# Routing weights of the expert rows: one-hot products on TensorE in place of a scatter and a reload

## The chip, the cores and the metric

The kernel runs on one NeuronCore of a Trainium2 chip. The metric is the device time of one execution in microseconds (us). Each core has five engines with a queue of their own: TensorE (PE in the profile; PEld is its weight load), VectorE (DVE), ScalarE (ACT), GpSimd (POOL) and SyncE (SP), which here only starts transfers. Engines wait for each other through semaphores; each works through its queue in order.

## The reference, cut to what matters

One encoder layer on 544 tokens (512 of one request, 32 of another): a mixer, then a mixture of experts on the normalised rows. The change touches only the second part.

```python
gl = t @ w_group + b_group                      # 4 groups
gp = softmax(gl); g_idx = top_k(gl, 1)
p_g = gp[g_idx]
el_sel = (t @ w_erouter[g_idx] + b_erouter)     # 4 experts of the group
top_v, top_i = top_k(el_sel, 2)
w2 = softmax(top_v) * p_g                       # two weights per token
expert_id = g_idx * 4 + top_i
combine = sum(one_hot(expert_id, 16) * w2[..., None])
for e in range(16):
    hid = silu(t @ w_gate[e]) * (t @ w_up[e])
    out = out + combine[:, e:e + 1] * (hid @ w_down[e])
```

Every token has two experts and two weights, `w1` and `w2` in the kernel. All is float32.

## The kernel before, in words

**Tiles.** The rows of one expert are gathered into a tile of 128 rows; an expert with more rows than that gets extra tiles. There are 16 tiles, one per expert, and up to 8 extra; `last`, read at run time, is the index of the last tile. Tile `i` has for each of its rows (a *slot*) a token and a routing weight. Tokens of slots are in `ids`, weights in `slot_w`, both with slots on the 128 partitions and tiles in the columns. The token of a slot is found by TensorE: VectorE makes a one-hot row of the token's rank within its tile (`at_rank`) and a one-hot of the tile times the token's number (`at_tile`, `at_extra`, all bf16), and the product of both over the tokens gives the numbers. The slot's weight goes another way: VectorE works out the address `w_at` = rank x 32 + tile (`weight_places`), POOL scatters the weights one element at a time to `w_dram` (the loop at L785 to L789, ten transfers: five token tiles times two choices), and after all have landed reloads the table into `slot_w` (L792). `w_dram` was zeroed early by a transfer of SP (L531).

**Work on a tile.** Weights of an expert come as six chunks of 1 MB (0, 1 gate; 2, 3 up; 4, 5 down). float32 products are made of three passes over rounded high and low parts (`three_passes`, L463), so for each chunk ACT makes the high part (`high_chunk`, L1089), VectorE the low part (`low_chunk`, L1988, 128x2048 elements), and when VectorE is done with a chunk SP loads the next tile's into the same place. For tile `i`:

- POOL: `gather(i)` fetches the tile's 128 rows (L767 copies the index, L762 sends the indirect transfer), once TensorE has transposed the tile before.
- TensorE: `turn_rows` transposes the gathered rows (L1509), `gate_up` makes gate and up products (48 matmuls), `turn_hidden` transposes the hidden rows (L1542), `down` makes the output rows (24 matmuls). `turn_rows(n)` and `turn_hidden` names count from tile 0, `turn_rows(1)` being tile 0's; `down(i)` is the down product of tile i - 1 and runs behind `gate_up(i)`.
- ACT: sigmoid of the gate (`gate`, L1112), high parts of transposed rows (L1098) and hidden rows (L1116), and `result(i)`: the output rows of tile i - 1 times `slot_w` (L1105), then a transfer of them to memory (L1108).
- VectorE: gate (L2114), `hidden` (L2119), low parts of rows (`rest_of_rows`, L2109) and of hidden rows (`rest_of_hidden`, L2123).

**What sets the order.** It is written out by hand for each engine. Tiles 0 and 1 are written out (`stage(0)`, `stage(1)`), tiles from 2 on run in a loop over `stage(i)`. Routing is finished while tiles 0 and 1 are under way: in VectorE's list `choice_weights` (the weights w1, w2), `extra_places`, `weight_places` and `extra_rows` stand between the chunks of tiles 0 and 1. In `stage(1)` ACT leaves `result(1)` out; it comes behind the stage, after a wait for the reload:

```python
            stage(1)
            act.wait_ge(w_moved, 16 * (2 * J + 1))
            result(1)
```

In the loop, `down(i)` on TensorE waits for `y_ready`, that is for ACT to have read the output rows of the tile before. At the end (L2194) VectorE waits for the reload once more, and POOL gathers every token's two rows and adds them to the residual (L806).

## Time and profile before

| | |
|---|---|
| median of 3 runs | 1048.53 us (1047.71 to 1052.13) |
| the profiled execution, its own time | 1052.81 us |
| its span, first to last instruction | 1050.7 us |
| mean granted clock of TensorE in it | 0.969 of full speed |
| busy: PE, DVE, ACT, POOL | 972.4, 674.0, 547.8, 288.1 us |
| chain that ended last, by engine | PE 43%, POOL 4%, DVE 3%, DMA 3% |
| of it, L788 (the scatter) and its reload | 2%, 1% |

A profile is one execution. Busy time says how long an engine worked, not whether anything waited for it. The idle time of an engine is put down to what ended it. The chain is followed back from the last instruction to what released each step. `PJ<-MEM_R 128*128 128x512` reads: written to PJ from MEM_R, 128 by 128 weights, 128 partitions by 512 elements.

### The profile page before, as it was taken

Reading aid. Unit: us, or ns where it says so; the run is one execution under the profiler, and the core shown is the slowest. Engines: PE = TensorE matmul, PEld = TensorE weight load, DVE = VectorE, ACT = ScalarE, POOL = GpSimd, SP = SyncE. Lnnn points to the kernel's source line nnn. Section 1 sums busy time; section 2 is a strip of 40 time slices with the busy share of each in tenths; the row PEclk is TensorE's granted clock in tenths of the full one; section 3 lists DMA queues with packets and bytes.
Section 4 is the critical chain, followed back from the end, with each engine's and each line's share of the span. In section 5 each row is a group of like instructions: output and inputs, shape, how many; then the busy total and the mean of one; then the engine's idle time right before and its main releaser. Section 6 shows DMA issues by size and latency. Waiting matters only on the chain.

```text
span 1050.7 us, 16726 instructions
## 1 busy us (share of the span) xinstructions
PE 972.4 (93%) x5963; PEld 856.7 (82%) x5963; DVE 674.0 (64%) x865; ACT 547.8 (52%) x610; POOL 288.1 (27%) x189
## 2 busy tenths in 40 slices
PE   5999899999999998899999999949779999999984
PEld 3999789889978986799999987737668888888873
DVE  5495659767865974622111114389598989898975
ACT  5645525825542572323333323457388787878752
POOL 1013214312421441533443443005400101011161
PEclk9999999999999999899999999969989999999998
DMA  9552222303222220233233269139899999999986
GB/s 294 172 169 70 53 57 60 105 20 91 79 59 58 58 76 4 61 86 95 80 85 94 80 206 310 61 135 315 330 356 396 413 413 414 412 412 413 384 205 171
DMA packets 146951, 193.20 MB, mean 184 GB/s; under 512 B 14936, under 2 KB 92158, under 8 KB 146788
## 3 DMA queue, kind: packets, MB, share of 16 engines
q1 hardware_dynamic: 139434, 166.34, 46.0%
q0 software_dynamic: 5008, 16.23, 5.2%
q10 hardware_dynamic: 2474, 10.18, 2.5%
q8 instruction: 21, 0.34, 0.1%
q14 instruction: 14, 0.11, 0.0%
HBM read 172.93 MB, written 19.79 MB: 183 GB/s over the span
## 4 chain that ended last, share of the span: by engine, by line
PE 43%; POOL 4%; DVE 3%; DMA 3%; issue 3%; SPq 2%; ACT 1%; ACTq 0%; DVEq 0%; POOLq 0%
PE PJ L463 40%; POOL slot_weights L788 2%; POOL MEM L806 2%; PE MS L1509 1%; SPq L609 1%; DMA MEM<-expert_rows,MEM 1%; PE NM L1457 1%; DMA MEM<-slot_weights 1%; PE NM L1542 1%; DMA RAW<-in_w_out_dram 0%; DMA MEM<-t_rows,MEM 0%; DVE MEM L2215 0%; POOL MEM_R L684 0%; DVE MEM_R L1988 0%; PE MS L1448 0%
## 5 line engine op out<-in xcount | busy, mean ns | idle before, releaser
L463 PE MATMUL PJ<-MEM_R 128*128 128x272 f32 (+2 forms) x5016 | 807.1, 322 | 11.6 <-DVE MEM_R L2109 3.4
L463 PEld LDWEIGHTS PJ<-MEM_R 128*128 128x128 f32 x5016 | 726.0, 192 | 75.7 <-issue 10.0
L684 POOL TENSOR_TENSOR MEM_R<-RAW,MEM_R 128x1024 fp32r<-128x1024 f32 x72 | 178.8, 2492 | 319.6 <-ACT MEM_R L831 319.6
L1988 DVE TENSOR_TENSOR MEM_R<-CHUNK,MEM_R 128x2048 fp32r<-128x2048 f32 x100 | 224.5, 2285 | 26.2 <-ACT MEM_R L1089 26.0
L1089 ACT CAST MEM_R<-CHUNK 128x2048 fp32r<-128x2048 f32 x100 | 189.3, 1912 | 12.5 <-PE PJ L463 8.0
L831 ACT CAST MEM_R<-RAW 128x1024 fp32r<-128x1024 f32 x81 | 84.3, 1048 | 130.4 <-DMA RAW<-in_w_pb_dram 42.9
L1901 DVE TENSOR_TENSOR MERGED<-PJ,MEM 128x544 f32<-128x544 f32 x16 | 11.6, 725 | 143.4 <-PE PJ L463 132.3
L767 POOL COPY MEM<-MEM 128x1 uint32 (+1 forms) x16 | 19.6, 1222 | 223.2 <-PE MS L1509 223.2
L1731 DVE SCALAR_TENSOR_TENSOR MEM<-MEM 128x548 f32<-128x548 f32 x72 | 58.9, 818 | 8.5 <-DVE MEM L1729 0.9
L1098 ACT CAST MEM_R<-MS 128x1024 fp32r<-128x1024 f32 x17 | 17.3, 1018 | 33.2 <-PE MS L1509 33.2
L888 ACT COPY MEM<-PJ 128x272 f32<-128x272 f32 x24 | 9.0, 376 | 45.8 <-PE PJ L463 45.8
L1105 ACT ACTIVATE MEM<-PJ,MEM 128x1024 f32<-128x1024 f32 x15 | 16.8, 1119 | 26.5 <-PE PJ L463 13.3
L895 ACT ACTIVATE MEM<-MEM 128x548 f32<-128x548 f32 x16 | 10.6, 664 | 38.1 <-DVE MEM L1731 38.0
L762 POOL DMA_INDIRECT MEM<-t_rows,MEM x18 | 19.3, 1075 | 26.4 <-POOL MEM L767 12.6
L1299 PE MATMUL MS<-MEM 128*128 128x512 f32 (+4 forms) x80 | 22.1, 420 | 4.5 <-DVE MEM L1771 4.4
L908 ACT ACTIVATE MEM<-NM 128x1024 f32<-128x1024 f32 x4 | 4.1, 1025 | 41.9 <-DVE M_Y L1805 41.9
L1745 DVE TENSOR_TENSOR MEM<-MEM 128x548 f32<-128x548 f32 x8 | 5.8, 730 | 30.4 <-ACT MEM L952 30.4
L1509 PE MATMUL MS<-MEM 128*128 128x128 f32 x136 | 18.5, 281 | 7.0 <-DMA MEM<-t_rows,MEM 7.0
L1509 PEld LDWEIGHTS MS<-MEM 128*128 128x128 f32 x136 | 16.5, 146 | 9.3 <-issue 7.4
L1299 PEld LDWEIGHTS MS<-MEM 128*128 128x128 f32 (+1 forms) x80 | 12.5, 189 | 14.0 <-DVE MEM L1771 7.7
L806 POOL DMA_INDIRECT MEM<-expert_rows,MEM x10 | 20.0, 1998 | 10.3 <-DMA expert_rows<-MEM 7.5
L1800 DVE SCALAR_TENSOR_TENSOR MEM<-MS,MEM 128x512 f32<-128x512 f32 x4 | 2.8, 692 | 30.4 <-PE MS L1327 30.4
(324 smaller groups left out, 947.2 us busy)
## 6 DMA issues: line engine op xcount, KB each, us to landing
CHUNK<-in_w_gate_dram SPq DMA_DIRECT2D x34, 1024.0 KB, 7.1
CHUNK<-in_w_up_dram SPq DMA_DIRECT2D x34, 1024.0 KB, 8.8
CHUNK<-in_w_down_dram SPq DMA_DIRECT2D x34, 1024.0 KB, 8.0
RAW<-in_w_in_dram SPq DMA_DIRECT2D x56, 512.0 KB, 3.7
expert_rows<-MEM ACTq DMA_DIRECT2D x15, 512.0 KB, 6.0
expert_rows<-MEM SPq DMA_DIRECT2D x10, 512.0 KB
RAW<-in_w_pa_dram SPq DMA_DIRECT2D x8, 512.0 KB, 3.6
RAW<-in_w_pb_dram SPq DMA_DIRECT2D x8, 512.0 KB, 3.6
```

The costliest lines, as they stand in the source:

```text
L463: ins = pe.matmul(out, w(a), x(b), start=first and n == 0, stop=last and n == 2)
L684: tt(lo, raw[slot], hi.bitcast(F32), ALU.subtract).then_inc(lo_done, 1)
L762: pool.indirect_dma_start(out=xg, out_offset=None, in_=t_dram, in_offset=bass.IndirectOffsetOnAxis(ap=index, axis=0)).then_inc(xg_in, 16)
L767: pool.tensor_copy(idcur[:, 0:1], ids[:, ds(col, 1)]).then_inc(steps_p, 1)
L788: pool.indirect_dma_start(out=w_dram, out_offset=bass.IndirectOffsetOnAxis(ap=w_at[0:n, m, j:j + 1], axis=0), in_=w[0:n, j:j + 1], in_offs ...
L806: pool.indirect_dma_start(out=x2[0:n, j, :], out_offset=None, in_=y_dram, in_offset=bass.IndirectOffsetOnAxis(ap=slot_i[0:n, m, j:j + 1], ...
L831: act.copy(hl[slot][0], raw[slot]).then_inc(hi_done, 1)
L1089: act.copy(moe_hl[c][0], moe_raw[c]).then_inc(chunk_hi[c], 1)
L1299: last = pe.matmul(b[0:rows_of[j], 0:n], k[:, ct, keys_of(j)], q[:, ct, quer], start=ct == 0, stop=ct == CT - 1)
L1509: last = pe.transpose(MS[:, half, P * m:P * m + P], xg[:, (4 * half + m) * P:(4 * half + m + 1) * P], ident)
L1731: ins = stt(dst, buf[:, tap:tap + LN_], cw[tap], dst, ALU.mult, ALU.add)
L1988: tt(moe_hl[c][1], moe_raw[c], moe_hl[c][0].bitcast(F32), ALU.subtract).then_inc(chunk_lo[c], 1)
```

## The change

The weights' table is made the way of the tokens' numbers. A weight is cut into three bf16 parts (its rounding, the rounding of what is left, and again), the one-hot of the tile is multiplied by each of the parts (`at_weight`, 3 x 26 columns for each token tile and choice), and ten bf16 matmuls with the one-hot of the rank (`at_place`) sum them over the tokens. VectorE adds the three parts up from PSUM into `slot_w`. The scatter, the reload, the table in memory, its zeroing and the addresses are gone.

- POOL makes the parts (five instructions of 10 elements, each waiting for the one before) and the three products, behind `stage(0)` and ahead of `stage(1)`.
- TensorE: `slot_weights`, behind `gate_up(1)`, ahead of `turn_rows(3)` and `down(1)`.
- VectorE: `is_tile` has 26 columns a token and choice instead of 10; `weight_places` goes; `place_weights` comes behind `low_chunk(5, 0)`.
- ACT: `result(1)` moves into `stage(1)`, ahead of `turned_hidden(1)`.
- TensorE's `down` no longer waits for `y_ready`: it waits for `hidT_ready`, which ACT and VectorE give only after `result`.
- `at_place` and `at_weight` lie where the output rows `yt` lie later.

```diff
+        w12 = small(2, J)
+        w1, w2 = w12[:, 0], w12[:, 1]
...
-        slot_w = small(WT)
+        slot_w = small(TAB)
...
-            sp.dma_start(w_dram.rearrange("(p t) a -> p (t a)", p=P), zeros[:, 0:WT]).then_inc(rows_zeroed, 16)
...
             stage(0)
-            pool.wait_ge(rows_zeroed, 16 * (EXTRA + 4))
+            pool.wait_ge(weights_ready, 1)
+            pool.tensor_copy(w_third[:, 0], w12).then_inc(w_split, 1)
+            pool.wait_ge(w_split, 1)
+            tt(w_left, w12, w_third[:, 0], ALU.subtract).then_inc(w_split, 1)
+            pool.wait_ge(w_split, 2)
+            pool.tensor_copy(w_third[:, 1], w_left).then_inc(w_split, 1)
+            pool.wait_ge(w_split, 3)
+            tt(w_left, w_left, w_third[:, 1], ALU.subtract).then_inc(w_split, 1)
+            pool.wait_ge(w_split, 4)
+            pool.tensor_copy(w_third[:, 2], w_left).then_inc(w_split, 1)
+            pool.wait_ge(w_split, 5)
             pool.wait_ge(weights_ready, 2)
-            for j in ORDER:
-                n = rows_of[j]
-                for m, w in enumerate((w1, w2)):
-                    pool.indirect_dma_start(out=w_dram, out_offset=bass.IndirectOffsetOnAxis(ap=w_at[0:n, m, j:j + 1], axis=0),
-                                            in_=w[0:n, j:j + 1], in_offset=None).then_inc(w_moved, 16)
+            for k in range(3):
+                tt(at_weight[:, :, :, k, :], is_tile, w_third[:, k].unsqueeze(3).to_broadcast([P, 2, J, TAB]), ALU.mult).then_inc(w_split, 1)
             stage(1)
-            pool.wait_ge(w_moved, 16 * 2 * J)
-            pool.dma_start(slot_w, w_dram.rearrange("(p t) a -> p (t a)", p=P)).then_inc(w_moved, 16)
...
-                if not isinstance(i, int):
-                    result(i)
+                if isinstance(i, int):
+                    act.wait_ge(weights_ready, 3)
+                result(i)
                 turned_hidden(i)
                 high_chunk(5, i)
 
             stage(1)
-            act.wait_ge(w_moved, 16 * (2 * J + 1))
-            result(1)
...
+            def slot_weights():
+                pe.wait_ge(w_split, 8)
+                for m in range(2):
+                    for j in range(J):
+                        n = rows_of[j]
+                        last = pe.matmul(NM[:, 1, 0:3 * TAB], at_place[0:n, m, j, :], at_weight[0:n, m, j].rearrange("p k t -> p (k t)"),
                                          start=m + j == 0, stop=m == 1 and j == J - 1)
                 last.then_inc(slots_done, 1)
...
-                if not isinstance(i, int):
-                    await_step(pe, y_ready, i)
                 pe.wait_ge(hidT_ready, i)
...
             gate_up(1)
+            slot_weights()
             turn_rows(3)
...
-                L(tt(is_extra, iox, spread2(t12, NX), ALU.is_equal))
+                L(tt(is_tile, iox, spread2(t12, TAB), ALU.is_equal))
+                dve.sem_inc(weights_ready, 1)
...
-            def weight_places():
-                L(stt(x12, r12, float(WT), t12, ALU.mult, ALU.add))
-                dve.tensor_copy(w_at, x12).then_inc(weights_ready, 1)
...
+            def place_weights():
+                dve.wait_ge(slots_done, 3)
+                dve.tensor_reduce(slot_w, NM[:, 1, 0:3 * TAB].rearrange("p (k t) -> p t k", k=3), AX.X, ALU.add).then_inc(weights_ready, 1)
...
-            weight_places()
             low_chunk(1, 1)
...
             low_chunk(5, 0)
+            place_weights()
...
-            dve.wait_ge(w_moved, 16 * (2 * J + 1))
```

What stands on three engines, with the lines of the respective kernel (a line of the kernel before moves down by 6 to 18 in the changed one). POOL's queue before, from the gather of `stage(0)` on:

```order
L767 COPY MEM<-MEM 128x1 [waits xT_full]
L762 DMA MEM<-t_rows,MEM 128x1024 [waits steps_p]
L788 DMA slot_weights<-MEM 4096x1 [waits weights_ready,rows_zeroed]
L788 DMA slot_weights<-MEM 4096x1 x9
L792 DMA MEM<-slot_weights 128x32 [waits w_moved]
```

Between the last two stand the copy and the gather of `stage(1)`, in rows like the first two. The same place in the changed kernel (W is `w_third`, SB is `at_weight`):

```order
L768 DMA MEM<-t_rows,MEM 128x1024 [waits steps_p]
L790 CAST W_66<-MEM 128x10 [waits weights_ready]
L792 TENSOR_TENSOR MEM<-MEM,W_66 128x10 [waits w_split]
L794 CAST W_66<-MEM 128x10 [waits w_split]
L796 TENSOR_TENSOR MEM<-MEM,W_66 128x10 [waits w_split]
L798 CAST W_66<-MEM 128x10 [waits w_split]
L802 TENSOR_TENSOR SB<-MEM,W_66 128x10x26 [waits weights_ready,w_split]
L802 TENSOR_TENSOR SB<-MEM,W_66 128x10x26 x2
L773 COPY MEM<-MEM 128x1 [waits xT_full]
```

Ten transfers and a reload have become eight instructions that read and write SBUF; the gather of `stage(1)` stands behind them as it stood behind the scatter. VectorE in the changed kernel, from `rest_of_rows(2)` to `hidden(1)` (L2005 is `low_chunk`, L2107 the new reduction):

```order
L2127 TENSOR_TENSOR MEM_R<-MS,MEM_R 128x1024 [waits xT_hi]
L2005 TENSOR_TENSOR MEM_R<-CHUNK_60,MEM_R 128x2048 [waits chunk_hi1]
L2005 TENSOR_TENSOR MEM_R<-CHUNK_61,MEM_R 128x2048 [waits chunk_hi2]
L2111 COPY MEM<-PJ 128x10 [waits slots_done]
L2112 TENSOR_TENSOR MEM<-PJ,MEM 128x10 [waits steps_v]
L2005 TENSOR_TENSOR MEM_R<-CHUNK_62,MEM_R 128x2048 [waits steps_v,chunk_hi3]
L2141 TENSOR_TENSOR MEM_R<-NM,MEM_R 128x512 [waits hT_hi]
L2005 TENSOR_TENSOR MEM_R<-CHUNK_63,MEM_R 128x2048 [waits chunk_hi4]
L2005 TENSOR_TENSOR MEM_R<-CHUNK_64,MEM_R 128x2048 [waits chunk_hi5]
L2107 TENSOR_REDUCE MEM<-NM 128x26 [waits slots_done]
L2005 TENSOR_TENSOR MEM_R<-CHUNK_59,MEM_R 128x2048 [waits chunk_hi0]
```

Before, two 10-element instructions stood ahead of the first L2005 row (then L1988), and the reduction was not there: now all of VectorE's work for tile 2 stands behind a wait for TensorE. ACT at the end of `stage(1)` in the changed kernel (L1116 is the output rows' scaling, L1127 `turned_hidden`, L1100 `high_chunk`):

```order
L1100 CAST MEM_R<-CHUNK_63 128x2048 [waits chunk_used4,chunk_in4]
L1116 ACTIVATE MEM<-PJ,MEM 128x1024 [waits y_out,weights_ready,chunk_used5]
L1119 DMA expert_rows<-MEM 128x1024 [waits y_ready]
L1127 CAST MEM_R<-NM 128x512 [waits hT_full]
L1100 CAST MEM_R<-CHUNK_64 128x2048 [waits chunk_used5,chunk_in5]
```

Before, the scaling and its transfer stood behind the last of these rows and waited for `w_moved`.

## Rows read from the trace of the kernel before

**Rows 1.** The head of the page.

```profile
span 1050.7 us, 16726 instructions
```

**Rows 2.** The chain that ended last, 748 to 799 us: start, us, what.

```profile
748.32 6.96 DMA MEM<-slot_weights
...
755.42 1.12 ACT MEM L1105
...
781.41 0.87 PE MS L1509 x8
782.28 5.58 PE PJ L463 x24
787.86 0.44 PE NM L1542 x4
788.29 10.91 PE PJ L463 x48
```

**Rows 3.** The waits of ACT from 690 us: total, times, longest (us).

```profile
ACT MEM L1105 <- DMA MEM<-slot_weights: 13.2, 1, 13.2
```

**Rows 4.** The timeline, TensorE: start, us, line, shapes, [idle before, releaser].

```profile
718.96 11.18 PE L463 MATMUL PJ<-MEM_R 128*128 128x512 f32 x48 [0.25 <-DVE MEM_R L2109]
...
739.16 0.66 PE L1542 MATMUL NM<-MEM 128*128 128x128 f32 x4 [2.58 <-DVE MEM L2119]
...
740.60 12.76 PE L463 MATMUL PJ<-MEM_R 128*128 128x512 f32 x48 [0.78 <-DVE MEM_R L2109]
...
755.26 1.06 PE L1509 MATMUL MS<-MEM 128*128 128x128 f32 x8 [1.90 <-DMA MEM<-t_rows,MEM]
...
756.83 5.83 PE L463 MATMUL PJ<-MEM_R 128*128 128x512 f32 x24 [0.51 <-ACT MEM L1105]
...
767.96 1.12 PE L1542 MATMUL NM<-MEM 128*128 128x128 f32 x4 [5.30 <-DVE MEM L2119]
```

**Rows 5.** Stretches: busy of PE, PEld, DVE, ACT, POOL, then clock, DMA share, GB/s.

```profile
740.60:753.40 12.80, 12.76 (x48) 10.07 (x48) 7.77 (x9) 1.64 (x1) 7.20 (x5) 0.87 1.04 405
753.40:756.80 3.40, 1.06 (x8) 0.86 (x9) 0.00 (x0) 1.11 (x1) 0.18 (x1) 1.00 0.36 143
756.80:762.70 5.90, 5.83 (x24) 4.44 (x24) 2.69 (x2) 4.63 (x4) 0.99 (x1) 1.00 0.54 178
762.70:769.00 6.30, 1.04 (x4) 0.72 (x4) 6.30 (x6) 6.30 (x5) 0.00 (x0) 0.66 0.82 275
...
781.50:800.00 18.50, 18.50 (x93) 15.45 (x91) 16.65 (x11) 14.28 (x10) 1.92 (x2) 1.00 1.04 406
```

**Rows 6.** The timeline, VectorE and POOL.

```profile
719.10 4.49 DVE L1988 TENSOR_TENSOR MEM_R<-CHUNK,MEM_R 128x2048 fp32r<-128x2048 f32 x2
...
722.46 1.87 POOL L788 DMA_INDIRECT slot_weights<-MEM  x1 [0.30 <-issue]
...
726.82 6.69 DVE L1988 TENSOR_TENSOR MEM_R<-CHUNK,MEM_R 128x2048 fp32r<-128x2048 f32 x3
...
727.47 2.48 POOL L788 DMA_INDIRECT slot_weights<-MEM  x1 [0.30 <-issue]
...
745.50 2.81 POOL L762 DMA_INDIRECT MEM<-t_rows,MEM  x1 [0.82 <-POOL MEM L767]
```

**Rows 7.** Single lines (ns min/median/max), then two matmul groups (us, mean ns).

```profile
L684 POOL TENSOR_TENSOR MEM_R<-RAW,MEM_R x72: 2345/2396/4055, 75.2 to 644.5; 128x1024 fp32r<-128x1024 f32 x72
L1731 DVE SCALAR_TENSOR_TENSOR MEM<-MEM x72: 787/790/2816, 53.6 to 370.5; 128x548 f32<-128x548 f32 x72
L767 POOL COPY MEM<-MEM x16: 181/1405/1407, 716.8 to 996.2; 128x1 uint32 x14, 128x1 uint32<-128x1 uint32 x2
L2070 DVE TENSOR_TENSOR MEM<-MEM x1: 253/253/253, 714.0 to 714.0; 128x100 f32<-128x100 f32 x1
...
L1501 PE MATMUL PJ<-AT 128*128 128x20 bf16 (+1 forms) x10 | 0.7, 174 | 0.0
L1484 PE MATMUL NM<-AT 128*128 128x80 bf16 (+4 forms) x5 | 0.5, 228 | 0.0
```

More of the change, by code:

```diff
@@ L82, in hawk_mlstm_hmoe_kernel @@
     TAB = TILES + 2
-    WT = 32
     EPS = 1e-6
@@ L121, in hawk_mlstm_hmoe_kernel @@
         y_dram = dram("expert_rows", [TILES * P + 1, D], F32)
-        w_dram = dram("slot_weights", [P * WT, 1], F32)
         rows_dram = dram("gate_rows", [2 * H * N + H * LS], F32)
@@ L303, in hawk_mlstm_hmoe_kernel @@
         lg, chosen = small(J, NR), small(J, NG, EG)
-        gmax, gidx, pg, w1, w2, dv = (small(J) for _ in range(6))
+        gmax, gidx, pg, dv = (small(J) for _ in range(4))
+        w12 = small(2, J)
+        w1, w2 = w12[:, 0], w12[:, 1]
         v12, i12, e12, r12, x12, q12, t12, a12 = (small(2, J) for _ in range(8))
@@ L328, in hawk_mlstm_hmoe_kernel @@
         assert bf0 + (J + 1) * NE <= 2 * 2 * N and NX <= NE
-        is_extra = late(J * D, 2, J, NX)
         slot_i = small(2, J).bitcast(U32)
@@ L332, in hawk_mlstm_hmoe_kernel @@
         last_i = small(1).bitcast(I32)
-        w_at = small(2, J).bitcast(U32)
-        slot_w = small(WT)
+        slot_w = small(TAB)
         sel_id = small(2)
+        is_tile = small(2, J, TAB)
+        w_left = small(2, J)
+        small(-o[0] % 8)
+        w_third = nc.alloc_sbuf_tensor_at("W3", [P, 6 * J], BF16, offset=base + 4 * (cuts["xh"] + o[0])).rearrange("p (k m j) -> p k m j", k=3, m=2)
+        small(3 * J)
+        s_words = nc.alloc_sbuf_tensor_at("SB", [P, 4 * N], BF16, offset=base + 4 * cuts["sig"])
+        at_place = s_words[:, 0:2 * J * P].rearrange("p (m j n) -> p m j n", m=2, j=J)
+        at_weight = s_words[:, 2 * J * P:2 * J * (P + 3 * TAB)].rearrange("p (m j k t) -> p m j k t", m=2, j=J, k=3)
+        assert 2 * J * (P + 3 * TAB) <= 4 * N
         ids = small(TAB).bitcast(U32)
@@ L797, in _ @@
                     stage(i)
-            pool.wait_ge(weights_ready, 3)
+            pool.wait_ge(weights_ready, 4)
             await_step(pool, y_out, last * 16)
@@ L1011, in _ @@
                 sigmoid_qk(hd, 3)
-                act.wait_ge(rows_zeroed, 16 * (EXTRA + 4))
+                act.wait_ge(rows_zeroed, 16 * (EXTRA + 3))
                 second_part(hd, (5,))
@@ L1106, in result @@
                                scale=slot_w[:, ds(i - 1, 1)]).then_inc(y_ready, 1)
-                act.wait_ge(y_ready, i + 1)
+                act.wait_ge(y_ready, i)
                 act.dma_start(y_dram[ds(i * P - P, P), :], yt).then_inc(y_out, 16)
@@ L1119, in _ @@
             act.sem_inc(y_out, 16)
-            act.sem_inc(y_ready, 1)
             turned_rows(1)
@@ L1500, in extra_slots @@
                         n = rows_of[j]
-                        last = pe.matmul(PJ[:, 2, 0:2 * NX], at_rank[m][0:n, j, :], at_extra[0:n, m, j, :],
+                        last = pe.matmul(PJ[:, 2, 0:2 * NX], at_place[0:n, m, j, :], at_extra[0:n, m, j, :],
+                                         start=m + j == 0, stop=m == 1 and j == J - 1)
+                last.then_inc(slots_done, 1)
+            def slot_weights():
[4 more added lines that the diff above has]
+                        last = pe.matmul(NM[:, 1, 0:3 * TAB], at_place[0:n, m, j, :], at_weight[0:n, m, j].rearrange("p k t -> p (k t)"),
                                          start=m + j == 0, stop=m == 1 and j == J - 1)
```

8 lines of the change are left out of this document (4 added, 4 removed).

## The prediction

> **What bounds the kernel now.** I read the page's head first, then the waits, then the chain that ended last, and last the timeline around the chain's odd stretch. The profiled execution took 1052.81 us, its span is 1050.7 [rows 1], so 2.1 us lie around the span; it is 4.3 above the median of the runs, 1048.53. A gain in the span is taken off the median as it stands.
>
> From tile 3 on TensorE does nothing but expert tiles, with no wait between them: gate_up 10.91, turn_rows 0.87, down 5.58, turn_hidden 0.44, together 17.80 us a tile [rows 2]. That part runs at TensorE's own pace and the change does not touch it. The odd stretch is ahead of it. ACT sits idle for 13.2 us until the routing weights have come back from memory [rows 3], and the reload alone is 6.96 us of the chain [rows 2]. ACT is in order, so all casts of the next tile stand behind that wait, VectorE's differences behind the casts, and hidden(2) behind those.
>
> What counts is what TensorE loses [rows 4]: 1.90 us before turn_rows(4), whose gather POOL issued late because it was still sending the scatter; about 0.5 before down(2); 5.30 before turn_hidden(2), which waits for hidden(2) on VectorE. After that the granted clock shows 0.66 for 762.7 to 769.0 [rows 5], that is a stretch at 1.2 instead of 2.4 GHz, and TensorE is through gate_up(3) only at 781.41 [rows 2]. An earlier stall, 2.58 and 0.78 us around turn_hidden(1), is caused by VectorE's backlog, not by the weights; behind it gate_up(2) takes 12.76 us [rows 4] where later ones take 10.91, at a mean clock of 0.87 [rows 5].
>
> **What is taken away.** Ten scatters and one reload leave POOL's queue, one zero fill leaves SP's, and with them ACT's 13.2 us. If nothing else moved, gate_up(2) would start at 740.60 as now, and TensorE would run through without waiting: 740.60 + 12.76 + 0.87 + 5.58 + 0.44 + 10.91 = 771.16 in place of 781.41, a gain of 10.2 us. I checked the cover: VectorE is through low_chunk(5, 1) at 747.4 and base_places at 748.6; three L1988 of 2.24 [rows 6] and two 512-column instructions of 0.7 put hidden(2) at 756.7, 16.1 us after gate_up(2) starts, and down(2) ends after 19.2. The zero fill was long finished and nothing waits for it by name: nothing. TensorE's wait for y_ready in down: its order is kept by hidT_ready, it stood idle for ACT once, 0.5 us, which is in the sum.
>
> **What is added, and where it stands.** POOL now splits w12 into three bf16 parts in five chained instructions of 10 elements, then makes three products of 260 elements. TensorE's ten matmuls (slot_weights) wait for the last product and stand ahead of turn_rows(3) and down(1). VectorE's place_weights waits for those matmuls and stands ahead of low_chunk(0, 2), so all of VectorE's work for tile 2 is behind it. Thus if POOL is late, both engines stop.
>
> Is POOL late? Row by row the scatters show when POOL gets at SBUF while VectorE runs L1988 (two inputs in SBUF). L1988 in a run of two from 719.10 ends at 723.59; the scatter begun at 722.46 ends at 724.33, 0.74 later. In the run of three from 726.82 a border lies near 729.06; the scatter begun at 727.47 ends at 729.95, 0.89 behind it [rows 6]. Seven of the other eight follow the same pattern; one, at 739.66, meets no L1988 and takes 0.97 in all. So a POOL instruction waits for the L1988 that is running and gets in at the border. The reverse is in the trace too: L1731 takes 790 ns but up to 2816, L684 on POOL 2396 but up to 4055 [rows 7]. By the Trainium skill, SBUF — State Buffer, section "SBUF: two separate sides", VectorE and GpSimd have one SBUF port pair in common, held as a lock for a whole instruction, the loser being blocked; by that rule the gain is cut, without it the 10.2 above would stand. The trace agrees, with the borders just given.
>
> The walk, in times of the trace before: POOL's gather(2) is issued by 718.7, then the chain starts. VectorE starts low_chunk(1, 1) about 718.9 (before at 719.10, since weight_places' two small instructions went) and runs five L1988 up to about 731.1, with short gaps for extra_rows and rest_of_hidden(0). Each of the five small POOL instructions is 0.18 us free and up to 1.41 when held [rows 7]. It gets in at a border (721.2, 723.4, 726.1, 728.9) or in one of the gaps, and either way the fifth is done by 728.9 to 729.1. A product: L684 is 2.34 ns an element, so 260 elements are 0.61 us; with the 0.18 of a tiny copy as its fixed part, 0.79 [rows 7]. Either the first product gets in at 728.9 and holds low_chunk(5, 0) back by 0.79, and the other two follow it, or all three start at 731.1; both end at 733.5. TensorE's ten matmuls of 78 columns lie between 174 ns each (20 columns) and 228 (80 columns, at the low clock) [rows 7]; issued back to back they overlap, and I take 0.8 for all: 734.3. VectorE's reduction of 78 elements is like the 0.25 of L2070 [rows 7]; done at 734.6 with its semaphore. low_chunk(0, 2) then starts near 734.7 instead of 731.3: **3.4 us late**. is_tile grows from 100 to 260 elements, some 0.15 us by the one nanosecond an element of VectorE, beside ACT's turned_rows(2), for which VectorE waits anyway: nothing.
>
> Who pays these 3.4 us: hidden(1), so turn_hidden(1) at 742.6 in place of 739.16, and gate_up(2) at 744.0 in place of 740.60. TensorE itself is ready earlier: 734.3 + 0.9 + 5.8 = 741.0 (gate_up(1) ends at 730.1 as before, 718.96 + 11.18 [rows 4]). ACT's result(1) now stands ahead of turned_hidden(1); it needs the end of down(1), 741.0, takes 1.12 [rows 2] and a DMA issue, and is done at 742.6, before turned_hidden(1) can start: hidden. POOL's gather(3) was issued from 745.50 on [rows 6] and its rows were used at 755.26 [rows 4], 9.8 later; now its copy can go at 735.3 and the gather some 2.2 later, so the rows are there by 747.3, and turn_rows(4) needs them at 756.8: hidden, the 1.90 us are gone.
>
> **Sum.** 10.2 - 3.4 = 6.8 us: gate_up(3) ends near 774.6. 1048.53 - 6.8 = **1041.7 us** (the profiled execution's own time: 1046.0, its span 1043.9). About 0.5%, 5.2 us, is what a measurement of this kernel tells from no change. Bounds: were POOL never held, 10.2, and 12.1 if the shorter stall before gate_up(2) also leaves the clock up (12.76 becomes 10.91). Downward: a product could take up to L684's full 2.4 us, if operands with repeated elements are slow; three add 4.8, which leaves 2.0. The new idle of TensorE, 730.1 to 733.5, may bring a low stretch of its own: 1.85 us by gate_up(2)'s excess, of which 1.6 is covered, since down(1) ends 1.6 ahead of hidden(1).
>
> **Rivals.**
> - *POOL is in time* (it finishes before 730, say because small instructions slip into gaps two at a time). Then gain 10.2 to 12.1: 1036.4 to 1038.3. For: the gap before low_chunk(3, 1) and the one at rest_of_hidden(0). Against: five chained plus three, and five L1988 in the way. Chance 0.17.
> - *The loads bound it.* In 740.6 to 753.4 the DMA share is 1.04 at 405 GB/s, as in 781.5 to 800 (1.04, 406). If loads set the pace, only idle DMA time can be won back: 0.64 x 3.4 + 0.46 x 5.9 + 0.18 x 6.3 = 6.0 us [rows 5], less the 3.4 by which VectorE frees buffers later: 2.6, so 1045.9. Against: TensorE waits for no load from 781 on, and its pieces add up to the period. Chance 0.10.
> - *The chain on POOL is longer than priced* (slow products). Gain 2.0 to 5, around 1045. Chance 0.13.
> - *Slower: the clock.* The new stall puts TensorE at 1.2 GHz and it stays there through down(1) and gate_up(2). down(1) ends near 746.8, gate_up(2) starts at 747.7 and takes 21.8 us (2 x 10.91): 769.5 against 756.8, 12.7 lost against 6.8 won, 1054.4. It decides if the low stretch outlasts down(1) by more than half of gate_up(2). Against: in gate_up(2) of before the mean is 0.87, so the low part is about a quarter of it [rows 5]. Chance 0.05.
> - *Forecast* as summed: 0.55.
>
> **How the numbers follow.** Faster by over 0.5% (below 1043.3): all of the first rival, 0.17, most of the forecast, 0.47 of 0.55, a little of the loads and the long chain, 0.06: 0.70. Within 0.5%: the rest of these, 0.25. Slower: 0.05. The range takes in the rivals but the last and the far ends: 1037.0 to 1046.0.
>
> **What would show it.** Right: no slot_weights DMA; ACT's 13.2 us wait gone; POOL's small instructions ending at the borders of VectorE's L1988, the last product near 733 to 734 when the start of gate_up(1) is laid on 718.96; TensorE idle 3 to 4 us before the 78-column matmuls; VectorE idle before its reduction; turn_hidden(2) with no wait. Wrong: the products done before gate_up(1) ends (gain of 10), products of over 1 us each free of VectorE (gain below 5), or a granted clock of 0.50 through all of gate_up(2).

## The result and the profile after

| | before | changed |
|---|---|---|
| median | 1048.53 us (1045.78 to 1052.45, 7 runs) | 1039.01 us (1036.23 to 1043.74, 7 runs) |
| the profiled execution | 1052.81 us | 1038.45 us |

The ratio is 0.9906, 95% interval 0.988 to 0.9932: 9.5 us between the medians, 7 to 12.6 by the interval. The forecast was 6.8 us and 1041.7, just outside that interval. The sign held, and so did the account of what is taken away; the size was short by a third, because the account of the cost failed. The head of the changed kernel's page:

```profile
span 1036.5 us, 16724 instructions
```

The spans differ by 14.2 us, more than the medians do. 3.8 of it lie ahead of gate_up(1), which started at 718.96 and now starts at 715.13. In the profiles of this study that start lies anywhere from 712.2 to 719.9, in kernels that differ little up to there, so I count from the start of gate_up(1) in each profile. TensorE's timeline of the changed kernel (start, us, line, shapes, idle time before it; L1519 is `slot_weights`, L1527 `turn_rows`, L1558 `turn_hidden`, L470 the products of `gate_up`, x48, and `down`, x24):

```profile
715.13 12.81 PE L470 MATMUL PJ<-MEM_R 128*128 128x512 f32 x48
727.78 0.84 PE L1519 MATMUL NM<-SB 128*128 128x78 bf16 x10
...
736.76 0.66 PE L1558 MATMUL NM<-MEM 128*128 128x128 f32 x4 [1.53 <-DVE MEM L2137]
738.20 11.16 PE L470 MATMUL PJ<-MEM_R 128*128 128x512 f32 x48 [0.78 <-DVE MEM_R L2127]
749.20 1.04 PE L1527 MATMUL MS<-MEM 128*128 128x128 f32 x8
749.99 5.83 PE L470 MATMUL PJ<-MEM_R 128*128 128x512 f32 x24
755.65 0.60 PE L1558 MATMUL NM<-MEM 128*128 128x128 f32 x4
756.17 11.19 PE L470 MATMUL PJ<-MEM_R 128*128 128x512 f32 x48
767.20 1.03 PE L1527 MATMUL MS<-MEM 128*128 128x128 f32 x8
```

Beside [rows 4]: the 1.90 us before turn_rows(4) and the 5.30 before turn_hidden(2) are gone (749.20 and 755.65 have no idle time), the 2.58 before turn_hidden(1) has become 1.53. gate_up(3) ends, and the transposes behind it start, 52.07 us after the start of gate_up(1); before it was 62.29. These are **10.2 us**, and from there to the end both profiles take the same (269.45 before, 269.30 now). So the whole gain lies in these two tiles, as forecast. It is a net figure, of one execution on each side: the one of before took 4.3 us more than its median.

ACT's waits from 686 us on:

```profile
ACT MEM L1116 <- PE PJ L470: 14.9, 15, 1.0
ACT MEM_R L1100 <- DMA CHUNK<-in_w_up_dram: 9.6, 14, 1.1
```

The 13.2 us of [rows 3] are gone. What is new is the second row: chunk loads now land 10 to 11.6 us after their issue in the median where it was 7 to 9, and ACT waits for one a tile, up to 1.1 us. Two tiles of the chain that ended last show that none of it reaches TensorE, whose 0.87, 5.58, 0.44 and 10.91 are those of [rows 2]:

```profile
802.98 0.87 PE MS L1527 x8
803.85 5.58 PE PJ L470 x24
809.43 0.44 PE NM L1558 x4
809.87 10.91 PE PJ L470 x48
```

Now the two queues on which the forecast's 3.4 us rested. POOL, from gather(2) to gather(3):

```profile
713.97 0.96 POOL L768 DMA_INDIRECT MEM<-t_rows,MEM  x1 [0.79 <-POOL MEM L773]
714.93 0.21 POOL L790 CAST W<-MEM 128x10 bf16<-128x10 f32 x1
715.22 2.14 POOL L792 TENSOR_TENSOR MEM<-MEM,W 128x10 f32<-128x10 f32 x1
717.43 2.13 POOL L794 CAST W<-MEM 128x10 bf16<-128x10 f32 x1
719.64 0.20 POOL L796 TENSOR_TENSOR MEM<-MEM,W 128x10 f32<-128x10 f32 x1
719.90 0.19 POOL L798 CAST W<-MEM 128x10 bf16<-128x10 f32 x1
720.18 5.76 POOL L802 TENSOR_TENSOR SB<-MEM,W 128x260 bf16<-128x260 f32 x3
...
731.94 2.83 POOL L768 DMA_INDIRECT MEM<-t_rows,MEM  x1 [0.79 <-POOL MEM L773]
```

and VectorE in the same time:

```profile
714.99 4.51 DVE L2005 TENSOR_TENSOR MEM_R<-CHUNK,MEM_R 128x2048 fp32r<-128x2048 f32 x2
719.43 0.15 DVE L2111 COPY MEM<-PJ 128x10 f32<-128x10 f32 x1
...
719.94 2.30 DVE L2005 TENSOR_TENSOR MEM_R<-CHUNK,MEM_R 128x2048 fp32r<-128x2048 f32 x1 [0.15 <-DVE MEM L2112]
722.16 0.68 DVE L2141 TENSOR_TENSOR MEM_R<-NM,MEM_R 128x512 fp32r<-128x512 f32 x1
722.76 5.32 DVE L2005 TENSOR_TENSOR MEM_R<-CHUNK,MEM_R 128x2048 fp32r<-128x2048 f32 x2
728.67 0.24 DVE L2107 TENSOR_REDUCE MEM<-NM 128x26 f32<-128x78 f32 x1 [0.58 <-PE NM L1519]
728.82 2.28 DVE L2005 TENSOR_TENSOR MEM_R<-CHUNK,MEM_R 128x2048 fp32r<-128x2048 f32 x1
```

L792 and L794 are held for 2.1 us each and end at the borders of the two L2005 from 714.99 (near 717.3 and 719.5), as forecast. But L790 got in before that pair began, and L796 and L798 both started in the half microsecond of L2111 and L2112, in which VectorE runs no instruction with two inputs in SBUF. The first product started 0.24 us too late for that gap:

```profile
720.18 2.55 POOL L802 TENSOR_TENSOR SB<-MEM,W 128x260 bf16<-128x260 f32 x1
```

It was held by the L2005 from 719.94. The second took 0.62 us beside L2141, which has an input in PSUM, and the third, 2.67 us, was held again. The three products end at 725.94, 10.8 us after gate_up(1) started; the forecast was 14.5. They hold VectorE's pair L2005 at 722.76 for 0.84 us in all (5.32 in place of 4.48). At 727.78 TensorE finds its operands waiting. VectorE idles 0.58 us for TensorE, not for POOL, and starts low_chunk(0, 2) 13.7 us after the start of gate_up(1), before 12.3: **1.4 us late, not 3.4**.

The clock: TensorE in slices of 1 us (length, busy, instructions, granted clock, DMA share, GB/s):

```profile
715.00:716.00 1.00, 1.00 (x7) 1.00 0.74 240
716.00:717.00 1.00, 1.00 (x4) 0.55 0.79 313
717.00:718.00 1.00, 1.00 (x4) 0.50 0.49 201
718.00:719.00 1.00, 1.00 (x4) 0.50 0.69 55
719.00:720.00 1.00, 1.00 (x5) 0.74 0.77 229
```

There is one stretch at 1.2 GHz, inside gate_up(1), which takes 12.81 us; gate_up(2) takes 11.16. Before it was the other way round, 11.18 and 12.76 [rows 4].

### The profile page after: what moved, and what is told of

It is laid out like the page before. It is cut to its first block, busy times and chain, and to the rows that moved or that the text cites. A ratio compares the mean times of both kernels' runs of the same rounds, so it can differ in the third digit from the quotient of the medians.

```text
span 1036.5 us, 16724 instructions
## 1 busy us (share of the span) xinstructions
PE 968.3 (93%) x5973; PEld 854.3 (82%) x5973; DVE 673.2 (65%) x864; ACT 548.6 (53%) x610; POOL 278.7 (27%) x186
## 4 chain that ended last, share of the span: by engine, by line
PE 72%; DVE 13%; issue 6%; ACT 4%; SPq 2%; DMA 2%; DVEq 1%; POOL 0%; ACTq 0%; POOLq 0%
PE PJ L470 60%; DVE MEM L1748 2%; PE NM L1326 2%; PE PJ L1275 2%; PE MS L1527 1%; DVE MEM L1849 1%; PE MS L1346 1%; PE MS L1308 1%; SPq L615 1%; DVE MEM_R L2005 1%; DMA MEM<-in_x_prompt_dram 1%; PE NM L1466 1%; PE NM L1558 1%; PE MS L1336 1%; DVE MEM_R L1658 1%
## 5 line engine op out<-in xcount | busy, mean ns | idle before, releaser
L470 PE MATMUL PJ<-MEM_R 128*128 128x272 f32 (+2 forms) x5016 | 804.4, 321 | 10.2 <-DVE MEM_R L2127 3.1
L470 PEld LDWEIGHTS PJ<-MEM_R 128*128 128x128 f32 x5016 | 723.8, 191 | 72.9 <-issue 9.0
L690 POOL TENSOR_TENSOR MEM_R<-RAW,MEM_R 128x1024 fp32r<-128x1024 f32 x72 | 176.2, 2455 | 318.9 <-ACT MEM_R L842 318.9
L2005 DVE TENSOR_TENSOR MEM_R<-CHUNK,MEM_R 128x2048 fp32r<-128x2048 f32 x100 | 225.4, 2293 | 15.6 <-ACT MEM_R L1100 14.3
L1100 ACT CAST MEM_R<-CHUNK 128x2048 fp32r<-128x2048 f32 x100 | 189.3, 1912 | 16.8 <-DMA CHUNK<-in_w_up_dram 9.6
L1918 DVE TENSOR_TENSOR MERGED<-PJ,MEM 128x544 f32<-128x544 f32 x16 | 11.6, 724 | 141.5 <-PE PJ L470 132.2
L773 POOL COPY MEM<-MEM 128x1 uint32 (+1 forms) x16 | 22.2, 1385 | 222.8 <-PE MS L1527 222.8
L768 POOL DMA_INDIRECT MEM<-t_rows,MEM x18 | 20.7, 1150 | 26.4 <-POOL MEM L773 12.6
L1116 ACT ACTIVATE MEM<-PJ,MEM 128x1024 f32<-128x1024 f32 x15 | 16.8, 1119 | 14.9 <-PE PJ L470 14.9
L1308 PEld LDWEIGHTS MS<-MEM 128*128 128x128 f32 (+1 forms) x80 | 12.3, 185 | 14.6 <-DVE MEM L1788 7.8
L1527 PE MATMUL MS<-MEM 128*128 128x128 f32 x136 | 18.6, 282 | 5.2 <-DMA MEM<-t_rows,MEM 5.2
L1527 PEld LDWEIGHTS MS<-MEM 128*128 128x128 f32 x136 | 16.5, 146 | 7.2 <-issue 5.3
## 6 DMA issues: line engine op xcount, KB each, us to landing
CHUNK<-in_w_up_dram SPq DMA_DIRECT2D x34, 1024.0 KB, 11.6
```

Of the source, the lines that this page charges most:

```text
L470: ins = pe.matmul(out, w(a), x(b), start=first and n == 0, stop=last and n == 2)
L690: tt(lo, raw[slot], hi.bitcast(F32), ALU.subtract).then_inc(lo_done, 1)
L768: pool.indirect_dma_start(out=xg, out_offset=None, in_=t_dram, in_offset=bass.IndirectOffsetOnAxis(ap=index, axis=0)).then_inc(xg_in, 16)
L773: pool.tensor_copy(idcur[:, 0:1], ids[:, ds(col, 1)]).then_inc(steps_p, 1)
L1100: act.copy(moe_hl[c][0], moe_raw[c]).then_inc(chunk_hi[c], 1)
L1308: last = pe.matmul(b[0:rows_of[j], 0:n], k[:, ct, keys_of(j)], q[:, ct, quer], start=ct == 0, stop=ct == CT - 1)
```

## The experiments

"Mark" is the time from the start of gate_up(1) to the transposes behind gate_up(3) in the run's profile; "turn" that to turn_hidden(1). The ratio is to the kernel before, run alongside; e1 and e5 do not compute the reference's output.

| run | median us | ratio to before, 95% interval | turn | mark |
|---|---|---|---|---|
| before | 1048.5 | | 20.20 | 62.29 |
| changed | 1039.0 | 0.9906 (0.988 to 0.9932) | 21.63 | 52.07 |
| changed, again | 1039.9 | 0.9907 (0.9882 to 0.9932) | 21.63 | 52.07 |
| e1 no wait on ACT | 1043.5 | 0.9934 (0.991 to 0.9957) | 20.20 | 56.64 |
| e2 result(1) behind stage(1) | 1039.1 | 0.9909 (0.9882 to 0.9936) | 20.96 | 54.08 |
| e3 chain ahead of stage(0) | 1041.8 | 0.9929 (0.9909 to 0.9949) | 21.47 | 53.31 |
| e4 products twice | 1042.2 | 0.9936 (0.9917 to 0.9955) | 23.90 | 54.33 |
| e5 half the scatters | 1039.0 | 0.9895 (0.9871 to 0.992) | 20.20 | 52.07 |
| e6 split on VectorE | 1041.9 | 0.9921 (0.9898 to 0.9944) | 22.14 | 54.78 |
| e7 slot_weights in the gap | 1039.9 | 0.991 (0.9882 to 0.9939) | 20.81 | 52.34 |
| e9 e7 and extra_slots earlier | 1040.5 | 0.9917 (0.9891 to 0.9944) | 20.82 | 52.33 |
| e10 e9 with filled gap | 1039.1 | 0.99 (0.9875 to 0.9926) | 21.42 | 51.40 |
| e11 scatter kept, wait moved | 1044.6 | 0.9962 (0.9944 to 0.998) | 20.21 | 54.47 |

The intervals are 4 to 6 us wide in all, so 1 us is told apart by the profiles alone, and each profile is one execution: that of e1 was the slowest of its seven (1049.42), that of e4 the fastest of its six (1039.32), that of e11 the second of twelve (1040.41). Theory A throughout: what was lost stood behind ACT's wait for the reload and behind POOL's queue of scatters; what is paid is the end of POOL's new chain, as far as it outlasts gate_up(1), and what VectorE does ahead of hidden(1).

### Where the loss was: e1, e5, e11

e1 keeps scatter and reload and takes ACT's wait away:

```diff
-                               scale=slot_w[:, ds(i - 1, 1)]).then_inc(y_ready, 1)
+                               scale=ones[:, ds(i - 1, 1)]).then_inc(y_ready, 1)
...
             stage(1)
-            act.wait_ge(w_moved, 16 * (2 * J + 1))
             result(1)
...
+            act.wait_ge(w_moved, 16 * (2 * J + 1))
             act.wait_ge(chunk_used[5], last)
```

> The kernel before, but output rows of all tiles save the last two are scaled by ones instead of the routing weights (so the output is not the reference's), and ACT waits for the reload only ahead of the last two tiles; the ten scatters and the reload stay on POOL. Theory A (the loss is ACT standing still for the reload, with all casts behind it): ACT's 13.2 us wait and TensorE's 5.3 us before turn_hidden(2) vanish, the 1.9 us before turn_rows(4) stay since POOL still sends its scatters first; gain over before 7 to 9 us, about 1040.5. Rival B (POOL's late gather or the scatters' traffic is the larger part): gain below 4 us, 1045 or more.

Measured: 0.9934, about 6.9 us, just below the 7 to 9 expected (4.5 to 9.5 by the interval); the mark is 5.65 us earlier than before, 4.6 later than in the changed kernel. TensorE's timeline of e1:

```profile
755.87 1.94 PE L1509 MATMUL MS<-MEM 128*128 128x128 f32 x8 [3.25 <-DMA MEM<-t_rows,MEM]
757.47 7.82 PE L463 MATMUL PJ<-MEM_R 128*128 128x512 f32 x24
```

The 5.3 us before turn_hidden(2) are gone. The wait for gather(3) is 3.25 us, longer than before's 1.90, because gate_up(2) was quicker here, and a low stretch of the clock follows it: 1.94 for transposes that take 1.03, 7.82 for a down that takes 5.83. So the late gather, which I priced at 1.90, costs 3.2 + 0.9 + 2.0 = 6.1 us here; less the 1.4 by which turn_hidden(1) is earlier than in the changed kernel, that is the difference of the marks. ACT's wait was the larger part of the loss, POOL's queue the rest. Rival B falls.

e5 leaves out the scatters of the second choice:

```diff
-                for m, w in enumerate((w1, w2)):
+                for m, w in ((0, w1),):
...
-            pool.wait_ge(w_moved, 16 * 2 * J)
+            pool.wait_ge(w_moved, 16 * J)
```

(and the two waits for the reload count J + 1 in place of 2 * J + 1).

> The kernel before, scattering only the weights of the first choice, so the rows of every second expert get weight zero (the output is not the reference's): five scatters instead of ten. Theory A (ACT and gather(3) wait for POOL's queue, about 2.3 us a scatter): POOL is free some 11.5 us earlier, gather(3) is in time, and the reload lands near the moment ACT is ready, so ACT's wait falls from 13.2 to about 2 us; most of the change's gain appears, 7 to 9 us, about 1041. Rival F (the loss sits in the reload's latency and the waits' order, not in the number of scatters): gain below 4 us.

Measured: 0.9895, 11 us (8.4 to 13.6 by the interval), more than the 7 to 9 expected. The mark, 52.07, is that of the changed kernel, but the equality is chance: turn_hidden(1) is 1.4 us earlier and gate_up(2) took 12.77 us in place of 11.16. ACT's waits, POOL's gather(3) and TensorE's timeline of e5:

```profile
ACT MEM L1105 <- DMA MEM<-slot_weights: 1.0, 1, 1.0
```

```profile
728.83 2.82 POOL L762 DMA_INDIRECT MEM<-t_rows,MEM  x1 [0.81 <-POOL MEM L767]
```

```profile
747.68 1.03 PE L1509 MATMUL MS<-MEM 128*128 128x128 f32 x8
748.47 5.83 PE L463 MATMUL PJ<-MEM_R 128*128 128x512 f32 x24
754.14 0.60 PE L1542 MATMUL NM<-MEM 128*128 128x128 f32 x4
```

No idle time before turn_rows(4) and turn_hidden(2). Nothing but five scatters has gone; scatter to memory, reload and the old order are all there. The method of the kernel before was not slow because it goes through memory. It was slow because ten scatters take 2.3 us each, held by L1988 as [rows 6] show, and gather(3) and the reload stand behind all ten: with five fewer, gather(3) is issued 15.4 us after the start of gate_up(1) (728.83 - 713.42) in place of 26.5, 11.1 us earlier, and of ACT's 13.2 us 1.0 is left. Rival F falls.

e11 keeps the scatter whole and moves ACT's wait into stage(2), behind the gate of tile 2 and three casts (the expectation says four):

```diff
+                if isinstance(i, int) and i == 2:
+                    act.wait_ge(w_moved, 16 * (2 * J + 1))
+                    result(1)
                 turned_rows(i + 2)
...
             stage(1)
-            act.wait_ge(w_moved, 16 * (2 * J + 1))
-            result(1)
+            stage(2)
...
-            with act.Fori(2, TILES) as i:
+            with act.Fori(3, TILES) as i:
```

> The kernel before with its scatter and reload, only that ACT's wait for the reload and result(1) stand in stage(2), behind four casts and the gate of tile 2 instead of ahead of them. Theory A (the loss is the work queued behind ACT's wait, and POOL's late gather beside it): TensorE's 5.3 us before turn_hidden(2) vanish, the 1.9 to 3.3 us before turn_rows(4) stay; gain over before 5 to 8 us, about 1043, near e1. Rival K (the weights must be there, wherever the wait stands): down(2) waits for result(1) as long as ACT did, gain below 3 us.

Measured: 0.9962, a gain of 4.0 us (2.1 to 5.9 by the interval) where 5 to 8 were expected, a miss; the profile's mark is 7.8 us earlier than before. TensorE's timeline of e11:

```profile
748.68 1.07 PE L1511 MATMUL MS<-MEM 128*128 128x128 f32 x8 [1.29 <-DMA MEM<-t_rows,MEM]
750.44 5.82 PE L463 MATMUL PJ<-MEM_R 128*128 128x512 f32 x24 [0.69 <-ACT MEM L1105]
756.10 0.60 PE L1544 MATMUL NM<-MEM 128*128 128x128 f32 x4
```

As expected the 5.30 is gone. 1.29 and 0.69 are left; 1.9 to 3.3 were expected before turn_rows(4), and the 0.69 before down(2) not at all. ACT still waits 2.4 us for the reload, and the later place has a price of its own: result(2) waits 3.6 us until result(1) has been sent from the same buffer, which held no matmul in this execution. The profile and the medians disagree by 3.8 us, for which I have no row: the profiled execution is one of the two quickest, and the others may hold longer waits. That the place of the wait matters is shown; how much of the gain a mere reordering brings is open between 2 and 8 us. Rival K, a gain below 3 us, is not excluded by the runs; its mechanism, down(2) waiting as long as ACT did, is not what the profile shows.

### What is paid: e4, e2, e6, e3

e4 makes the three products a second time, into the same place, and TensorE waits for the second set:

```diff
-            for k in range(3):
+            for n, k in enumerate((0, 1, 2) * 2):
+                if n == 3:
+                    pool.wait_ge(w_split, 8)
                 tt(at_weight[:, :, :, k, :], is_tile, w_third[:, k].unsqueeze(3).to_broadcast([P, 2, J, TAB]), ALU.mult).then_inc(w_split, 1)
...
-                pe.wait_ge(w_split, 8)
+                pe.wait_ge(w_split, 11)
```

> The changed kernel with the three products made twice, the second set behind the first and TensorE waiting for it. Theory A (the end of POOL's chain is the price: both TensorE and VectorE wait for it): the chain ends near 15 us after the start of gate_up(1) instead of 10.8, VectorE starts low_chunk(0, 2) 2 to 2.5 us later, TensorE idles before the 78-column matmuls; 2 to 4 us slower than the changed kernel, about 1041.5. Rival E (hidden anyway, the stall before turn_hidden(1) swallows it): within 0.5 us of it.

Measured: 0.9936, 3.1 us slower than the changed kernel by the ratios. TensorE's timeline of e4:

```profile
726.88 1.12 PE L1521 MATMUL NM<-SB 128*128 128x78 bf16 x10 [3.46 <-POOL SB L804]
727.93 1.97 PE L1529 MATMUL MS<-MEM 128*128 128x128 f32 x8
729.55 6.21 PE L470 MATMUL PJ<-MEM_R 128*128 128x512 f32 x24
736.14 0.66 PE L1560 MATMUL NM<-MEM 128*128 128x128 f32 x4 [0.37 <-DVE MEM L2139]
```

This is the case that the prediction described: the chain ends 14.6 us after the start of gate_up(1), TensorE idles 3.46 us for POOL, turn_hidden(1) is 2.3 us later than in the changed kernel, and the mark too. So what the prediction put behind the end of the chain is right for a chain of that length; in the changed kernel the chain was shorter. Rival E falls. The idle spell also brings a low stretch, but it lies in the ten matmuls, the transposes (1.97) and the start of down(1) (6.21), where the wait before turn_hidden(1) covers it, as the prediction had it.

e2 undoes the other part of the change: result(1) behind stage(1), and down's wait for y_ready (with the counts of y_ready that go with it).

```diff
-                if isinstance(i, int):
-                    act.wait_ge(weights_ready, 3)
-                result(i)
+                if not isinstance(i, int):
+                    result(i)
...
             stage(1)
+            act.wait_ge(weights_ready, 3)
+            result(1)
...
+                if not isinstance(i, int):
+                    await_step(pe, y_ready, i)
```

> The changed kernel with result(1) back behind stage(1) and down's wait for y_ready back; the weights still come by TensorE. Theory A (availability of the weights matters, not the place of result(1)): the weights are there about 13.5 us after gate_up(1) starts, result(1) then stands 4 us later on ACT without any wait for weights; time within 1.5 us of the changed kernel, 1038 to 1041. Rival C (half of the gain is the moved result and the dropped wait): 3 us or more slower than the changed kernel, 1042 or more.

Measured: 0.9909, the same as the changed kernel. Its mark is 2.0 later, but because gate_up(2) met the low stretch and took 14.07 us; there is no idle time before down(2). turn_hidden(1) is 0.7 us earlier, since gate_up(1) took 11.19 us here. The place of result(1) and the dropped wait are worth nothing that these runs can tell. Rival C finds no wait in the profile; the interval alone, some 5 us wide, does not quite exclude its 3 us.

e6 moves the five splits and the products to VectorE, behind rest_of_rows(2):

```diff
             rest_of_rows(2)
+            split_weights()
             low_chunk(1, 1)
```

where split_weights holds POOL's eight instructions, with VectorE's own steps between them.

> The changed kernel with the five splits and the three products on VectorE, behind rest_of_rows(2), instead of POOL. Theory A (VectorE is the late engine up to turn_hidden(1), POOL has time): VectorE's own work grows by 5 x 0.2 + 3 x 0.42 = 2.3 us, the 0.84 us in which POOL held low_chunk goes, so turn_hidden(1) starts 1 to 1.5 us later; 1 to 2.5 us slower than the changed kernel. Rival G (the shared use of SBUF costs more than the instructions themselves): as fast or faster than the changed kernel.

Measured: 0.9921, 1.5 us slower than the changed kernel beside it. TensorE's timeline of e6:

```profile
721.22 8.45 PE L470 MATMUL PJ<-MEM_R 128*128 128x512 f32 x36 [1.20 <-DVE MEM_R L1991]
...
739.11 1.12 PE L1544 MATMUL NM<-MEM 128*128 128x128 f32 x4 [2.15 <-DVE MEM L2132]
```

low_chunk(1, 1) is late and TensorE stops inside gate_up(1) for 1.20 us, which I had not thought of; turn_hidden(1) comes 0.5 us later than in the changed kernel, where 1 to 1.5 were expected. The rest of the later mark is gate_up(2), 13.58 us with a low stretch. So the work costs VectorE somewhat more than POOL's holding costs it, by the 0.5 us of one profile; rival G is not borne out, but the difference in the ratios, 1.5 us, lies within the intervals.

e3 puts the whole chain ahead of stage(0):

```diff
+            pool.wait_ge(weights_ready, 1)
+            pool.tensor_copy(w_third[:, 0], w12).then_inc(w_split, 1)
...
+                tt(at_weight[:, :, :, k, :], is_tile, w_third[:, k].unsqueeze(3).to_broadcast([P, 2, J, TAB]), ALU.mult).then_inc(w_split, 1)
             stage(0)
```

> The changed kernel with POOL's five splits and three products ahead of stage(0) instead of behind it. Theory A (VectorE's L1988 and POOL exclude each other in SBUF): the chain starts before gate_up(1), ends within 4 us of its start instead of 10.8 behind it, holds no low_chunk of tile 0 any more (the pair that took 5.3 us takes 4.5), VectorE starts low_chunk(0, 2) some 0.8 us earlier; 0.5 to 1.5 us faster than the changed kernel, about 1038, and gather(2), later by the chain's 3 us, costs nothing. Rival D (the late gather(2) now holds turn_rows(3)): slower by 1 us or more.

Measured: 0.9929, 2.4 us slower than the changed kernel, a miss. The pair of low_chunk was not held any more (4.48), as expected. But VectorE's one-hot instructions, which stand ahead of hidden(0), were. VectorE's timeline of e3:

```profile
710.36 1.15 DVE L2091 TENSOR_TENSOR SB<-MEM 128x640 bf16<-128x640 f32 x1
711.44 0.68 DVE L2092 TENSOR_TENSOR AT<-MEM 128x100 bf16<-128x100 f32 x1
712.04 1.24 DVE L2091 TENSOR_TENSOR SB<-MEM 128x640 bf16<-128x640 f32 x1
```

In the changed kernel these take 0.82, 0.26 and 0.82. hidden(0) comes 1.2 us later, TensorE waits 2.42 us for it instead of 1.23, and gate_up(1) starts that much later. The other 1.2 us are in the mark: gate_up(1) took 12.65 us and gate_up(2) 12.75, both with a low stretch. The 0.8 us expected at low_chunk(0, 2) became 0.2 (13.5 us after the start of gate_up(1) in place of 13.7), since VectorE now waited 1.30 us for TensorE ahead of its reduction. gather(2) was later as well, and nothing waited for it: rival D had the sign right and the place wrong.

### TensorE's idle time and the clock: e9, e10, e7

e9 moves matmuls into idle time; e7 is e9 without its first part:

```diff
-            turn_hidden(0)
             extra_slots()
+            turn_hidden(0)
             gate_up(1)
-            slot_weights()
             turn_rows(3)
             pe.wait_ge(extra_ready, 1)
             down(1)
+            slot_weights()
             turn_hidden(1)
...
             low_chunk(5, 0)
-            place_weights()
...
                 rest_of_rows(i + 2)
+                if isinstance(i, int):
+                    place_weights()
```

> The changed kernel with extra_slots ahead of turn_hidden(0), slot_weights behind down(1) and VectorE's reduction behind rest_of_rows(3). Theory A (TensorE waits for VectorE at turn_hidden(0) and turn_hidden(1), and VectorE pays 0.6 us of waiting and the reduction ahead of hidden(1)): the matmuls move into idle time, turn_hidden(1) starts 0.8 us earlier, and with shorter idle spells some low stretch of the clock (1.6 us each) can go; 1 to 3 us faster than the changed kernel. Rival H (the reload's successor, result(1), now gets its weights later than ACT needs them, and turned_hidden(1) behind it holds rest_of_hidden(1)): no faster or slower.

> The changed kernel with slot_weights behind down(1) and the reduction behind rest_of_rows(3), extra_slots left where it is. Theory A: turn_hidden(1) starts 20.8 us after gate_up(1) starts as in e9 (21.6 in the changed kernel), unless a low stretch of the clock falls in gate_up(1) and down(1) ends later; time within 1.5 us of the changed kernel, not to be told from it. Rival L (moving TensorE's small matmuls into idle time is worth the 0.8 us and a low stretch): 2 us faster or more.

Measured: 0.9917 and 0.991. turn_hidden(1) started 0.8 us earlier in both (20.8), as expected, and then gate_up(2) took 12.47 and 12.45 us. Neither is told apart from the changed kernel; for e7 that was expected, for e9 it is a miss. Rival H had the number of e9 but not the cause: no idle time stands before down(2), and gate_up(2) was slow by its clock.

e10 issues slot_weights' matmuls of e9 three times over:

```diff
-                for m in range(2):
+                for m in (0, 1) * 3:
```

> The kernel of e9 with the ten matmuls of slot_weights issued three times over (the same product into the same place), so that TensorE's idle spell before turn_hidden(1) shrinks from 2.5 to about 0.8 us. Theory I (the low stretch of the clock in gate_up(2), 12.5 us instead of 11.2, answers to that idle spell): gate_up(2) takes 11.2 us and the kernel is 1 to 1.5 us faster than e9, about 1039. Rival J (the low stretch only moves to another place, as it did between the two profiles of the changed kernel and the others): some other group is 1 to 2 us longer and the time is that of e9 within 1 us.

Measured: 0.99. TensorE's timeline of e10:

```profile
715.91 12.80 PE L470 MATMUL PJ<-MEM_R 128*128 128x512 f32 x48 [0.47 <-DVE MEM_R L2127]
...
735.00 2.40 PE L1519 MATMUL NM<-SB 128*128 128x78 bf16 x30
737.33 0.66 PE L1558 MATMUL NM<-MEM 128*128 128x128 f32 x4
738.13 11.16 PE L470 MATMUL PJ<-MEM_R 128*128 128x512 f32 x48
```

The gap before turn_hidden(1) is filled, gate_up(2) takes 11.16, and gate_up(1) takes 12.80, with 0.47 us of idle time before it. Each side is half right: gate_up(2) went to 11.2 us as theory I has it, and another group became 1.6 us longer as rival J has it. The time, 1.8 us below e9 by the ratios, lies within the intervals of both. Its mark, 51.40, is the earliest of all, and the time is not to be told from the changed kernel's. No version here that computes the reference's output is faster than the changed kernel beyond doubt.

The changed kernel once more:

> The changed kernel once more, beside the other three. Theory A: the low stretches of the granted clock fall differently from run to run while the waits stay; gate_up(1) or gate_up(2) may take 11.2 or 12.8 us, and turn_hidden(1) still starts 20.4 to 21.7 us after gate_up(1) starts. Median within 2 us of 1039.

Measured: 1039.85 us, 0.9907, with the same low stretch in gate_up(1) (12.81 us) and the same mark. The waits stayed, as expected, but the low stretch did not fall differently: between these two profiles of the same kernel nothing in this stretch moved.

## Why the prediction was right, and where its size was off

The number came out inside the stated range, and the sign and what is taken away were right. The cost was not: of the signs that the prediction names for being right, the last product near 733 to 734 and TensorE idle for 3 to 4 us before the 78-column matmuls did not appear, and the first sign for being wrong did, products done before gate_up(1) ends (725.94 against 727.94).

- **What is taken away: 10.2 us.** Right. Without the cost of 1.4 and the 1.6 us by which gate_up(2) was quicker, the profiles show 10.2 + 1.4 - 1.6 = 10.0. That the net gain of the profiles is 10.2 as well is chance: cost and quicker gate_up(2) nearly cancel. e5 shows that the loss was the length of POOL's queue, e1 that ACT's wait was the larger part of it.
- **The walk on POOL.** This is the step that failed: "either way the fifth is done by 728.9 to 729.1 ... both end at 733.5". Laid on the trace of before, the fifth was done at 723.9 and the products at 729.8, 3.7 us earlier. Three things were mis-sized. The first instruction got in before VectorE's pair began, by 0.06 us. The fourth and the fifth fell into one gap, since a free POOL instruction here takes 0.2 us and the next follows 0.06 to 0.09 behind; I had let a gap take one at most, although the first rival names it, and gave that rival 0.17. And the three products were neither held once and then in a row nor 0.79 us each: the first and the third were held for an L2005 each (2.55 and 2.67 us), and the second, which was not held, took 0.62.
- **What it costs: 3.4 us.** Measured 1.4: the products hold VectorE for 0.84, the reduction takes 0.24, and 0.58 is a wait for TensorE, which was late because of its clock; 0.28 come back since the pair of low_chunk starts earlier. In e2, where gate_up(1) took 11.19 us, the cost is 0.8. In e4, where the chain has the forecast's length, TensorE waits for POOL and the cost is 3.7.
- **gate_up(2) at 12.76 us.** It took 11.16; the low stretch lay in gate_up(1), where most of it was hidden by the wait before turn_hidden(1). I kept the stretch in its place and named its going as a bound. That it moved is luck for the size and not shown to be an effect of the change: in e2 it lies in gate_up(2) again. The forecast's mark is 62.29 - 6.85 = 55.4, the measured one 52.07; the 2.0 us of the point above and the 1.6 of this one make up the 3.4, to 0.2.
- **Hidden at no cost.** gather(3) (issued at 731.94, no wait at 749.20), result(1) ahead of turned_hidden(1), the dropped y_ready (e2), the zero fill: right. is_tile: VectorE's idle time before turned_rows(2)'s result did not cover all of it; with a step's wait of 0.15 it came to 0.28 us at turn_hidden(0) (1.23 of idle time, before 0.95), and gate_up(1) was not moved by it.
- **The loads bound it.** Wrong by TensorE's unbroken 17.80 us a tile, but the loads are nearer to being the bound than before: ACT now waits for a chunk in each tile.
- **Slower by the clock.** The new idle spell did not arise; where it did, in e4, the low stretch was over within down(1).
- **Range and chances.** 1039.01 lies between the forecast and the first rival (1036.4 to 1038.3). By the rival's own condition, products done before 730 on the trace of before (729.8), the rival is what happened: POOL was in time. It had 0.17, the forecast 0.55; the time still fell between the two, by less than the interval can tell apart, with 1.4 us of cost in it.

## What to carry to other kernels

Small transfers issued from POOL are instructions in a queue with a price each (here 2.3 us beside VectorE's two-input work), and an in-order engine that waits for the last of them holds everything behind its wait; before replacing the method, look at which instructions are queued behind the wait and how many issues are ahead of the awaited one (e5 and e11). When work is moved to an engine that shares SBUF access with a busy one, lay its instructions one by one on the other's timeline, gaps included: the order in which they meet decides, and moving the chain to an idle-looking place (e3) put it against the instructions on the critical path.
